# Order of loads, mixer row and quarter sum between the first layer's mixer and its gate/up products

## The reference

```python
def even_mixer(h, conv_buf, S0, w_in, conv_w, lb, gnorm, w_out):
    ...
    o = rmsnorm(o, gnorm) * jax.nn.silu(gp.astype(F32).reshape(N, T, HG_HEADS, HG_DK))
    b_out = o.reshape(N, T, HG_WIDTH).astype(h.dtype)
    y = jnp.concatenate([a_out, b_out], axis=-1) @ w_out

def swiglu(h, w_gu, w_down):
    g, u = jnp.split(h @ w_gu, 2, axis=-1)
    return (jax.nn.silu(g) * u) @ w_down

        xp = xp + mp[2] * yp                               # gated residual
        hp = modulate(xp, norm_ffn[l], mp[3], mp[4])       # rmsnorm, scale, shift
        xp = xp + mp[5] * swiglu(hp, w_gu[l], w_down[l])
```

## Time and profile before

| | us |
|---|---|
| median of 3 runs | 2901.68 |
| lowest, highest | 2895.94, 2910.32 |
| the profiled execution | 2908.53 |
| its span | 2906.9 |
| TensorE busy in it | 2809.2 (97%) |
| VectorE, GpSimd, ScalarE busy | 1293.4, 1093.9, 793.5 |

### The profile page before, as it was taken

The page is one execution under the profiler, slowest core; times in us unless marked ns, Lnnn a source line. Parts: engine busy times, 40 slices in busy tenths (PEclk is TensorE's granted clock), DMA queues, the critical chain, the costliest instruction groups (busy, mean ns, idle before and its releaser), DMA issues.

```text
span 2906.9 us, 58706 instructions
## 1 busy us (share of the span) xinstructions
PE 2809.2 (97%) x21633; PEld 2607.3 (90%) x21633; DVE 1293.4 (44%) x2593; ACT 793.5 (27%) x1769; POOL 1093.9 (38%) x1156
## 2 busy tenths in 40 slices
PE   6999999898999999999889999999999999999999
PEld 5888999798999999999877787878789999999999
DVE  4767678565333343423466566666640110201103
ACT  5121211345444443000543242323351001010014
POOL 4000000356555564333744333333274343343344
PEclk9999999999999999999999999999999999999999
DMA  7422111534555535631233524242521111111112
GB/s 263 132 74 95 38 38 45 183 119 144 175 183 193 189 109 193 227 105 40 62 116 104 162 80 158 84 157 86 161 77 43 44 51 47 47 44 41 53 43 82
DMA packets 312485, 311.46 MB, mean 107 GB/s; under 512 B 22499, under 2 KB 266582, under 8 KB 310886
## 3 DMA queue, kind: packets, MB, share of 16 engines
q1 hardware_dynamic: 290450, 275.91, 29.4%
q10 hardware_dynamic: 13652, 24.63, 2.4%
q0 software_dynamic: 8192, 8.40, 1.1%
HBM read 254.50 MB, written 54.38 MB: 106 GB/s over the span
## 4 chain that ended last, share of the span: by engine, by line
PE 88%; DVE 3%; ACT 3%; SPq 2%; POOL 2%; DMA 2%; issue 1%; DVEq 0%; POOLq 0%; ACTq 0%
PE bank L3279 23%; PE bank L3280 22%; PE bank L3281 22%; PE bank L3887 2%; PE bank L4006 2%; PE bank L3908 2%; PE bank L3408 1%; PE bank L3929 1%; PE bank L3570 1%; PE bank L3542 1%; PE bank L3994 1%; PE bank L3587 1%; SPq L702 1%; PE bank L3876 1%; POOL hl L1093 1%
## 5 line engine op out<-in xcount | busy, mean ns | idle before, releaser
L3279 PE MATMUL bank<-hh,whi 128*128 128x344 f32 (+2 forms) x2380 | 782.7, 329 | 35.7 <-POOL wlo L1064 7.1
L3281 PE MATMUL bank<-hh,wlo 128*128 128x344 f32 (+2 forms) x2380 | 764.0, 321 | 0.0
L3280 PE MATMUL bank<-hl,whi 128*128 128x344 f32 (+2 forms) x2380 | 764.0, 321 | 0.0
L3279 PEld LDWEIGHTS bank<-hh,whi 128*128 128x128 f32 x2380 | 454.3, 191 | 61.4 <-issue 19.4
L3280 PEld LDWEIGHTS bank<-hl,whi 128*128 128x128 f32 x2380 | 454.4, 191 | 2.3 <-issue 1.0
L3281 PEld LDWEIGHTS bank<-hh,wlo 128*128 128x128 f32 x2380 | 454.5, 191 | 0.5
L1062 POOL CAST whi<-wst 128x1024 fp32r<-128x1024 f32 (+5 forms) x180 | 129.9, 721 | 726.6 <-PE bank L3281 485.7
L3279 PE MATMUL bank<-t_high,op_h 128*128 128x258 f32 x1232 | 354.0, 287 | 8.5 <-ACT u L1829 4.2
L3280 PE MATMUL bank<-t_low,op_h 128*128 128x258 f32 x1232 | 349.8, 284 | 0.0
L3281 PE MATMUL bank<-t_high,op_l 128*128 128x258 f32 x1232 | 348.1, 283 | 0.0
L1064 POOL TENSOR_TENSOR wlo<-wst,whi 128x1024 fp32r<-128x1024 f32 (+5 forms) x180 | 283.0, 1572 | 14.4
(11 more groups left out here) (454 smaller groups left out, 5084.5 us busy)
## 6 DMA issues: line engine op xcount, KB each, us to landing
pk<-in_cache_ckv SPq DMA_DIRECT2D x256, 128.0 KB, 2.4
ada_x<-in_w_ada SPq DMA_DIRECT2D x28, 1024.0 KB, 7.4
wst<-in_w_gu SPq DMA_DIRECT2D x44, 512.0 KB
raw<-in_w_gu SPq DMA_DIRECT2D x42, 512.0 KB, 4.6
wst<-in_w_in_even SPq DMA_DIRECT2D x28, 512.0 KB
wst<-in_w_down SPq DMA_DIRECT2D x32, 384.0 KB
down_high<-act_high SPq DMA_DIRECT2D x22, 516.0 KB, 5.9
down_low<-act_low SPq DMA_DIRECT2D x22, 516.0 KB, 6.6
```

What stands on the lines that cost most here:

```text
L3279: mm(out, wh_, xh_, start=start, stop=False, skip_group_check=more)
L3280: mm(out, wh_, xl_, start=False, stop=False, skip_group_check=more)
L3281: return mm(out, wl_, xh_, start=False, stop=stop, skip_group_check=more)
```

## The change

Nothing is computed differently except that two instructions' columns are cut and one step changes its engine.

- SP's queue: each row's weights are requested as soon as its staging tile is free, ahead of the x pieces and of the first gate/up weights (raw_first), which now come last.
- The last mixer row is worked in pieces 0 to 344, 344 to 516, 516 to 688 and 688 to 1032 (`LAST_ROW`). The first two end the mixer; the others follow residual 3 on VectorE and square 3 on ScalarE. ScalarE's table load comes before the squares, and its casts of rows 2 and 3 before those of the mixer row. The root of chunk 1 goes to rt, the squares' sum to a tile of its own (acc_part), since the old places are still in use.
- Second half of the projection: rows 0, 6, 7, 1 in quarter 2 and 0, 1, 6, 7 in quarter 3 (before 0, 1, 6, 7 in both). The third quarter's sum is put between matmuls 12 and 13 of part 28, its reciprocal and scaling one residual earlier.
- First gate/up unit: ScalarE makes all eight first_high before the fourth quarter's sum, and the casts of P7, P4 and P3 after it; GpSimd's lows for these three move behind first_low 4 to 7. Row tiles 2 and 3 of there_shifted are done by VectorE. u3_copy(0) and p1_copy(1) move forward between the sums' casts; P5 of q = 1 goes ahead of P3 of q = 0 on TensorE; t3 comes before c22(0), and g1(0) only after both lows of VectorE; gate1(0) now stands behind u2_copy(1) and ahead of u3_copy(1).

```diff
-PARTS += [(m, n) for m in (4, 5) + KEPT_ROWS[:2] for n in (2, 3)] + [(m, n) for n in (2, 3) for m in KEPT_ROWS[2:] + (6, 7)]
+PARTS += [(m, n) for m in (4, 5) + KEPT_ROWS[:2] for n in (2, 3)] + [(m, 2) for m in (0, 6, 7, 1)] + [(m, 3) for m in (0, 1, 6, 7)]
...
+LAST_ROW = [(0, 0, CW), (1, CW, 2 * QW), (None, 2 * QW, 2 * CW), (2, 2 * CW, N)]
...
+                weights(2)
+                keep(0)
                 x_part(0)
+                weights(3)
+                keep(1)
                 x_part(1)
-                weights(2)
-                weights(3)
-                keep(0)
-                keep(1)
-                x_part(2)
...
+                weights(5)
+                keep(3)
+                weights(6)
+                x_part(2)
+                weights(7)
...
-                weights(5)
-                keep(3)
-                weights(6)
-                weights(7)
...
-                for c in range(NC):
-                    low_half(HI_OUT + ROWS0 * NC + c, ROWS0, c, xT[:, ROWS0, cols(c)])
+                for c, start, stop in LAST_ROW:
+                    if c is None:
+                        pool.wait_ge(hi_ready, HI_LAT)
+                    else:
+                        pool.wait_ge(hi_ready, HI_OUT + ROWS0 * NC + c + 1)
+                    ins = nc.gpsimd.tensor_tensor(hl[:, ROWS0, start:stop], xT[:, ROWS0, start:stop], hh[:, ROWS0, start:stop].bitcast(F),
+                                                  ALU.subtract)
+                    if c is not None:
+                        ins.then_inc(lo_ready, 1)
...
-                adds(HALF + 7, HALF + 13)
+                adds(HALF + 7, HALF + 12)
...
-                op_low(P7, first)
+                adds(HALF + 12, HALF + 13)
+                first_low(1, 0)
+                first_low(1, 1)
                 adds(HALF + 13, HALF + 14)
-                op_low(P4, first)
+                first_low(1, 2)
+                first_low(1, 3)
                 adds(HALF + 14, HALF + 15)
-                op_low(P3, first)
...
-                acc = acc_row[:, quarter_cols(n)]
+                acc = acc_part[:, quarter_cols(n)]
...
-                for k in range(KT):
+                for k in range(KH, KT):
                     first_low(1, k)
+                for p in (P7, P4, P3):
+                    op_low(p, Unit(0, 0))
...
+                table(1)
                 head_norm(HEADS - 1)
-                for c in range(NC):
-                    act.wait_ge(y_ready, NC * (HEADS - 1) + c + 1)
-                    high(hh[:, ROWS0, cols(c)], xT[:, ROWS0, cols(c)])
...
-                table(1)
+
+                def last_row(c, start, stop):
+                    act.wait_ge(y_ready, NC * (HEADS - 1) + (2 if c is None else c) + 1)
+                    ins = nc.scalar.copy(hh[:, ROWS0, start:stop], xT[:, ROWS0, start:stop])
+                    if c is not None:
+                        ins.then_inc(hi_ready, 1)
+
+                last_row(*LAST_ROW[0])
+                last_row(*LAST_ROW[1])
...
+                    if p == 3:
+                        last_row(*LAST_ROW[2])
+                        last_row(*LAST_ROW[3])
...
+                quarter_root(2)
...
-                quarter_root(2)
-                act.wait_ge(*part_done(HALF + 13))
-                op_high(P7, first)
-                part_square(HALF + 13)
-                op_high(P4, first)
-                op_high(P3, first)
...
-                part_square(HALF + 14)
+                part_square(HALF + 13)
...
+                part_square(HALF + 14)
+                for k in range(KH, KT - 1):
+                    first_high(1, k)
                 part_square(HALF + 15)
-                first_high(1, 4)
+                first_high(1, KT - 1)
                 quarter_root(3)
+                op_high(P7, first)
...
-                for k in range(5, KT):
-                    first_high(1, k)
-                for k in range(KH):
-                    there_shifted(1, k)
+                op_high(P4, t)
+                op_high(P3, t)
+                there_shifted(1, 0)
+                there_shifted(1, 1)
...
-                sum_high(P3, 1)
...
-                sum_high(P6, 1)
-                sum_high(P7, 1)
-                sum_high(P4, 1)
-                gate1(0, t)
+                for p in (P3, P6, P7, P4):
+                    sum_high(p, 1)
...
+                gate1(0, t)
+                u3_copy(1, t)
...
-                u3_copy(1, t)
...
+            def gated_out(h, c, start, stop, more=False):
+
+                w, at = stop - start, slice(start - c * CW, stop - c * CW)
+                dve.wait_ge(hrt_ready, NC * h + c + 1)
+                order(v.reciprocal(rs[:, 0:w], root_in(h, c)[:, at]))
+                dve.wait_ge(bank_free[c], G_IN + 7 * h + SLOT_G + 2)
+                order(v.scalar_tensor_tensor(oacc[:, start:stop], oacc[:, start:stop], gnT, rs[:, 0:w], ALU.mult, ALU.mult))
+                y = xT[:, h + HEADS, start:stop]
+                ins = v.tensor_tensor(y, y, oacc[:, start:stop], ALU.mult)
+                if more:
+                    order(ins)
+                else:
+                    ins.then_inc(y_ready, 1)
+
+            def head_tail(h):
+
+                outputs_in(h)
...
-                    dve.wait_ge(hrt_ready, NC * h + c + 1)
-                    order(v.reciprocal(rs[:], hsq[c]))
-                    dve.wait_ge(bank_free[c], G_IN + 7 * h + SLOT_G + 2)
-                    order(v.scalar_tensor_tensor(oacc[:, cols(c)], oacc[:, cols(c)], gnT, rs[:], ALU.mult, ALU.mult))
-                    y = xT[:, h + HEADS, cols(c)]
-                    v.tensor_tensor(y, y, oacc[:, cols(c)], ALU.mult).then_inc(y_ready, 1)
+                    gated_out(h, c, c * CW, (c + 1) * CW)
...
-                for p in range(HALF):
-                    if p == 4:
-                        dve.wait_ge(x_back[1], 16)
-                    elif p == 14:
+                part_low(2)
+                part_residual(0)
+                part_residual(1)
+                part_low(3)
+                part_residual(2)
+                part_residual(3)
+                gated_out(HEADS - 1, 1, LAST_ROW[2][1], LAST_ROW[2][2], more=True)
+                gated_out(HEADS - 1, 2, *LAST_ROW[3][1:])
+                part_low(4)
+                dve.wait_ge(x_back[1], 16)
+                for p in range(4, HALF):
+                    if p == 14:
...
-                    if p in (0, 1, 3, 4, 6, 8):
-                        part_low({0: 2, 1: 3, 3: 4, 4: 5, 6: 6, 8: 7}[p])
+                    if p in (4, 6, 8):
+                        part_low({4: 5, 6: 6, 8: 7}[p])
...
-                for p in range(HALF + 9, HALF + 13):
+                for p in range(HALF + 9, HALF + 12):
...
-                part_residual(HALF + 13)
+                part_residual(HALF + 12)
...
+                scaled(2, 1)
+                part_residual(HALF + 13)
                 part_residual(HALF + 14)
-                scaled(2, 1)
...
+                for k in (2, 3):
+                    x = xT[:, k, 3 * QW:T]
+                    order(v.tensor_scalar(x, x, a[:, k, 0:1], shift[:, k, 0:1], ALU.mult, ALU.add))
...
+                t3(1)
                 c22(0, t)
-                g1(0, t)
-                t3(1)
...
+                g1(0, t)
...
-                    row(p, 0, KT).then_inc(part_done(p)[0], 1)
+                    if p == HALF + 12:
+                        row(p, 0, KH)
+                        quarter_sum(2)
+                        row(p, KH, KT).then_inc(part_done(p)[0], 1)
+                    else:
+                        row(p, 0, KT).then_inc(part_done(p)[0], 1)
...
-                    elif p == HALF + 12:
-                        quarter_sum(2)
...
+                pe.wait_ge(*quarter_free(KT))
+                first(P5, 1)
                 first(P3, 0)
-                pe.wait_ge(*quarter_free(KT))
-                for p in (P5, P6, P7, P4, P3):
+                for p in (P6, P7, P4, P3):
```

21 lines of the change are left out of this document (13 added, 8 removed).

## The result

The changed kernel takes 2886.98 us (median of 6 runs, 2884.51 to 2893.09), the kernel before on the same chip 2906.72 (6 runs, 2895.94 to 2910.32). The ratio of the mean times is 0.9943, with a 95% interval of 0.9925 to 0.9961: 16.6 us faster, between 11 and 22 (the two medians lie 19.7 apart). A second chip gave 0.9943 again (0.993 to 0.9957). The forecast was 2881.6 with a range of 2873 to 2892, and "faster by over 0.5%" with 0.76. So the direction and the range held. Whether the gain is over the 14.5 us that the prediction called faster is not settled by the times, as their interval begins at 11.

A forecast was written before the change was run, and what follows sets the result against it. TensorE, busy 97% of the span, was taken as the bound, so only its waits and low clock could go. Terms 8.3 + 5.8 + 2.5 + 3.5 = 20.1 us off the median 2901.7 gave 2881.6, range 2873 to 2892.

The forecast's parts named there:

- The budget: TensorE, 540 to 710 us: 21.3 us of waits plus 4.8 of low clock, 26 us that the edit could touch.
- The last mixer row: Mixer row's end before part 4: half-chunk work starts part 4 6.7 us earlier and saves 1.6 of clock, 8.3 us.
- rival B: Part 9: weight row 5 stays late, the 5.8 us fall to about 0, time 2887.4; chance 0.14.
- The queue: SP's queue, weight rows first: part 9's wait for row 5 and its low clock go, 5.8 us.
- Row 1 last: Part 25 becomes part 27: its whole wait for row 1's return goes, 2.5 us.
- The third sum and the pair: Third quarter's sum inside part 28 and reordered first gate/up pair: second unit 4.4 us earlier; 3.5 us counted.
- with the durations of before: First gate/up pair: steps after the fourth sum were timed with the earlier trace's durations, t4 3.48 us, two lows 5.45.
- Rival A: First pair: GpSimd and VectorE hinder each other, lows at 2.24 us each, pair's end slips 2 to 3, 2884.2; chance 0.16.
- Rival C: First pair gives nothing or less, -1 us instead of 3.5, time 2886.1; chance 0.12.
- Rival D: First gate/up weights, last in SP's queue, land late and stop TensorE at residual 11; slower, 2916; chance 0.03.
- The base: Starting time for the forecast: 2901.7 us, median of three runs lying 14 us apart; gain taken from it.
- The promised signs: Trace signs at parts 4, 9 and 16, no kept_lo wait, about 1 us at fourth sum, 2.3 and 1.7 at P4, P3.

The follow-up runs named there:

- row_only: Kernel before with the last mixer row alone worked half by half (queue, parts and first pair as before); ratio 1.0027, 1.0012 to 1.0042.
- second profile: The changed kernel profiled once more, nothing altered, beside the combined one on one chip; ratio to the kernel before 0.9943, 0.9930 to 0.9957.
- lows_on_vectore: Changed kernel with GpSimd's three sum lows of half 1 done by VectorE, some ScalarE copies ahead of casts; ratio to the kernel before 0.9949.

## Why the prediction was right, and where not

**The budget** named the right places: of 21.3 us of waits 13.1 went, and the low clock at parts 4 and 9.

**The last mixer row, 8.3 forecast, 7.4 measured** (5.9 at part 4, and 1.5 of clock by part 5). The steps came out nearly as written: the first reciprocal starts 0.8 earlier (0.9 was written), and half a chunk takes 2.2 us against 1.9. The miss is GpSimd's low of the half chunk: 1.10 us instead of about 0.5, because VectorE's weight low had begun at 545.06. TensorE waits 0.78 for it.

```profile
545.06 1.22 DVE L2676 TENSOR_TENSOR wx_lo<-wst,wx_hi 128x1024 fp32r<-128x1024 f32 x1
```

```profile
545.59 1.10 POOL L1126 TENSOR_TENSOR hl<-xT,hh 128x172 fp32r<-128x172 f32 x1 [1.01 <-ACT hh L1669]
```

The second half of the row cost TensorE nothing, as forecast: part 8 and part 9 start without a wait, and rival B fell.

**The queue, 5.8 forecast, 6.0 measured.** ScalarE casts row 4 at 555.09 and row 5 at 558.81 without waiting for a transfer, against the earlier trace rows:

```profile
555.09 1.04 ACT L1743 CAST whi<-wst 128x1024 fp32r<-128x1024 f32 x1
...
558.81 1.03 ACT L1743 CAST whi<-wst 128x1024 fp32r<-128x1024 f32 x1
```

Part 16 comes 13.4 us earlier; 14.1 was forecast. But the prediction took the two terms as independent, and row_only shows that they aren't. The sum was right since both edits were made; a reader who had taken the first term alone would have got the sign wrong.

**Row 1 last, 2.5 forecast, 2.8 measured.** In the first profile 0.6 of it is given back by a new wait for row 0's return, in the second 0.7 by the third sum. "No wait for kept_lo" was wrong by 0.37 us.

**The third sum and the pair, 3.5 forecast, -0.3 to 0 measured.** This is the step that failed, and with it goes nearly the whole difference. Set to the end of P1 of half 0, the pair's steps came late one by one. The last square ends 0.7 us later than written, so the fourth sum waits 1.5 and not 0.8. Samples and rows 2 and 3 on VectorE end 2.2 us later, 1.4 of it new. t4 ends 3.7 later, 1.4 more by t3, which I carried over with 1.47 us and which took 3.24. The second unit starts 4.3 later (3.9 in the second profile), against the 4.4 that the step promised. The cause of the two terms of 1.4 is the step "with the durations of before": it kept VectorE's durations although the new order puts these instructions beside GpSimd's. The samples' two operations now stand beside the weight lows. And t3 now begins with GpSimd's low of P5 (645.59 and 645.50, shown under lows_on_vectore) and waits for all of it. In the kernel before it was issued when most of that low was over, so its 1.47 held only the rest of the wait:

```profile
668.92 1.47 DVE L2679 TENSOR_TENSOR xT<-xT 128x1032 f32<-128x1032 f32 x1
```

```profile
666.99 2.31 POOL L1176 TENSOR_TENSOR t_low<-xT,t_high 128x1032 fp32r<-128x1032 f32 x1 [4.46 <-ACT t_high L1779]
```

The 3.48 us of t4 and the 5.45 of the two lows in the earlier trace rows had such waits in them already; taken as durations they hid them.

**Rival A** had the right pair of engines and the wrong victim: it charged GpSimd's three weight lows with 2.24 us each. They took 1.27 (3.82 for three), and VectorE's small operation beside them took 1.21 instead of 0.23. Its price, 2.6 us on the time, was near the 2.8 of the two steps. **Rival C** (the pair gives -1, 2886.1) is nearest to what happened, with A's mechanism as its reason. **Rival D** did not appear: raw_first was waited for 0.4 us.

**The base.** The three runs shown first had a median of 2901.7; six had 2906.7. 20.1 us off the latter would be 2886.6, next to the measured 2887.0, but that is luck: the trace and the ratio both say 15.4 to 16.6.

The promised signs: part 4 within 0.5 us (shown), part 9 without wait (shown), part 16 at 14 us (13.4), fourth sum about 1 us (1.5), P4 of half 1 2.3 and P3 1.7 (0.9 and 0.35 in the first profile, where low clock stretched P7 and covered them; 1.7 and 1.6 in the second, without it). P7 ahead of them waited 2.5 us for VectorE's low, where 0.95 was written.

## What to carry to other kernels

When an edit moves work of GpSimd beside work of VectorE, price both anew: a VectorE instruction with two SBUF operands and a GpSimd subtraction wait for each other's whole instruction, so their durations add up. Giving such work to VectorE, which here does it in about half the time (1.23 us against 2.25), can shorten the chain even though VectorE is the engine that bounds it. Edits that look like separate terms may need each other: build each alone before adding their gains. And where executions of one kernel differ by 10 us of low clock, compare the starts of the same instruction from a point just ahead of the edit, not spans.
